# Layer-norm statistics of the mix in a hybrid encoder layer: from bn_stats and a ScalarE normalisation to an accumulator, ScalarE squares and two scalar_tensor_tensor ops

## Chip, cores and metric

The kernel runs on one core of one Trainium2 chip, in float32. The metric is the device time of one execution in microseconds (us). Three runs of the kernel before gave 1359.98, 1362.23 and 1364.86 us; the median is 1362.23 us.

## The reference

One encoder layer over 1536 tokens of width 1024: one sequence of 512 and one of 1024, each with its own conditioning rows (shift, scale, gate). Cut to what matters:

```python
h = x * (1 + sc1) + sh1
mix = token_mixer(h, ...)                         # ends in a product with w_out
x = layer_norm(ALPHA * x + g1 * mix, ln1_g, ln1_b)   # the part that is changed
h = x * (1 + sc2) + sh2
y = hierarchical_moe(h, ...)                      # 32 experts, top-1 group, top-2 experts
return layer_norm(ALPHA * x + g2 * y, ln2_g, ln2_b)

def layer_norm(x, g, b):
    mu = mean(x); xc = x - mu; var = mean(xc * xc)
    return xc * rsqrt(var + LN_EPS) * g + b
```

## The kernel before

The tokens are 12 tiles of 128 rows. Five stages follow one another: conditioning and the first product (to about 325 us), the mix stage that is changed here (about 325 to 516 us), routing tables (to about 560 us), the experts (to about 1275 us), and a last stage that adds the two expert outputs and makes the second layer norm. Every product is split into a high and a low part, so that one float32 product is three matmuls (`three`, L1554 to L1556).

In the mix stage each engine has its own program, and all orders are written out by hand. For tile t:

- **TensorE (PE).** `mix(t)` makes 2 halves (b = 0, 1) of 8 x 3 matmuls of 512 columns each into two PSUM banks; it waits for `z2_l_made`. From tile 2 on, `h2_transposes(t-2)` (L1745) stand between the two halves and wait for `h2_ready`. Behind `mix(t)` comes `route(t-2)` (L1767), which waits for `logit_read`, that is, until VectorE has read the logits of tile t-3. Between `mix(1)` and `mix(2)` stands `edge_mm(6)` (L1649), which sets `fb_made` to 2.
- **VectorE (DVE).** `norm_tile(t)` is `second(t)`, then `low_z(t+2)` (L1255, the low part of the input of `mix(t+2)`), then `x1_out(t)`, then `logits_out(t-2)` (L1328). `second(t)` multiplies both halves by the gate (L1304), adds the residual (L1307, waits for the load of `xr`), takes bn_stats of both halves (L1310), joins them (L1312), adds epsilon (L1314), waits for GpSimd's power, and makes -mean * rstd (L1316, `nmr`).
- **ScalarE (ACT).** `high_z(t+2)` (L881), `normalise(t)` (L938), `copy_h2T(t-1)` (L946).
- **GpSimd (POOL).** `second(t)` makes rstd by a power (L682, one element a row), then waits for x1 and makes h2 = x1 * (1 + sc2) + sh2 in two ops of 1024 elements (L690, L692). Before the first power it waits for `fb_made` to be 2, and between tile 0 and tile 1 it has one more op of 1024 elements (L696).
- **SP (DMA queue).** It loads `xr` of tile t (L531) when the residual of tile t-1 has been taken, and stores h2 and x1 (L535, L537) when h2 is ready. For tile 4, with which the second sequence begins, the load stands behind the stores of tile 3.

The semaphores of the changed part run in this order before: `res_ready` (L1307), `var_ready` (L1314), `rstd_ready` (L682), `shift_ready` (L1316), `res_normed` (L938), `x1_ready` (L1323), `h2_ready` (L692).

The last stage already holds the other form of the same layer norm: L1518 adds the residual with an accumulator, L1520 makes the negative mean, ScalarE squares with that bias (L1063), L1524 makes the variance, GpSimd the power (L776), and L1528 and L1533 normalise.

Of the kernel before, what the change touches and what calls it, by code (L numbers as in the profile page):

```python
# [25 lines left out]
ACT = mybir.ActivationFunctionType  # L26
ALU = mybir.AluOpType
AX = mybir.AxisListType

P = 128  # L30
D = 1024
KD = D // P
# [13 lines left out]
EPS = 1e-5  # L46
ALPHA = 2.0 ** 0.25
# [60 lines left out]
def encoder(nc, ins, outs):  # L108
    ctx = ExitStack()
    with ctx:  # L110
        names = []

        def sem(name):
            names.append(name)
            return ctx.enter_context(nc.semaphore(name))
# [23 lines left out]
        r = Region(W0)  # L139
        win_h = r.take("win_h", [P, KD, 3 * AW], F32R)  # L140
        win_l = r.take("win_l", [P, KD, 3 * AW], F32R)
        r = Region(W0)
# [5 lines left out]
        r = Region(W0)  # L148
# [7 lines left out]
        r = Region(Z0)  # L156
# [7 lines left out]
        r = Region(Z0 + 32 * KB)  # L164
        win_raw = [r.take(f"win_raw{s}", [P, 3 * AW]) for s in range(2)]
        r = Region(C0 + 1312 + 4 * KD * PT * 2)
# [3 lines left out]
        r = Region(Z0 + 24 * KB)  # L170
# [4 lines left out]
        r = Region(Z0)  # L175
        z2T = r.take("z2T", [P, NP, KD, PT])
        r = Region(Z0)
        x1 = r.take("x1", [P, NT, D])

        r = Region(C0)  # L180
# [4 lines left out]
        r = Region(TOP0)  # L185
# [10 lines left out]
        r = Region(C1)  # L196
# [32 lines left out]
        v_rstd = r.take("v_rstd", [P, 1])  # L229
        edge_i = r.take("edge_i", [P, EDGE])  # L230
        edge_w = r.take("edge_w", [P, 2, len(WINDOWS), EDGE])
        stat = r.take("stat", [P, 2, 6])
        mv = r.take("mv", [P, 2])
        rstd = r.take("rstd", [P, 1])
        nmr = r.take("nmr", [P, 1])
# [4 lines left out]
        r = Region(C1)  # L240
# [5 lines left out]
        ln_g = r.take("ln_g", [P, D])  # L246
        ln_b = r.take("ln_b", [P, D])
        w_mid = Region(W0).take("w_mid", [P, KD, 3, AW])
        g1b, sc2b, sh2b = [[b[:].rearrange("p (a n) -> p a n", a=2), w_mid[:, 2 * j:2 * j + 2, 1, :]] for j, b in enumerate((g1b, sc2b, sh2b))]
        xr = Region(XS0).take("xr", [P, D])  # L250
        res = Region(V0).take("res", [P, D])
# [3 lines left out]
        r = Region(C1)  # L255
# [38 lines left out]
        r = Region(C0)  # L294
# [14 lines left out]
        r = Region(W0)  # L309
# [30 lines left out]
        def bcast(row, n):  # L340
# [10 lines left out]
        S = {n: sem(n) for n in (  # L351

            "c_loaded rows_loaded small_loaded sp_rows_loaded wsp_loaded ident_made c_silu cT_made c_ready c_low mod_init"
            " colsT_made cols_ready wspT_made wspT_ready rowsum_made rowsum_ready off_made off_ready"
            " edge_iota spl_ones"

            " x_loaded xT_made x0_ready ada_h_made ada_l_made ada_made mod_hl_made mod_cols mod_made"
            " k_mod k_high k_low win_h_made win_l_made h_ready hT_h_made hT_l_made"
            " late_h_made late_l_made late_made late_row added_h added_l g2_loaded g2_made g2_row g2_added"
# [419 lines left out]
        def _(act):  # L779
# [155 lines left out]

            def normalise(t):
                act.wait_ge(S["shift_ready"], t + 1)
                nc.scalar.activation(res[:], res[:], ACT.Identity, scale=rstd[:, 0:1], bias=nmr[:, 0:1]).then_inc(S["res_normed"], 1)  # L938

            def copy_h2T(t):  # L940

# [6 lines left out]

            high_z(2, 0, 1)
            normalise(0)  # L950
            high_z(3, 1, 1)
            normalise(1)
            copy_h2T(0)
            with act.Fori(1, NT // 2 - 2) as i:
                for s in range(2):
                    high_z(2 * i + s + 2, s, i + 1)
                    normalise(2 * i + s)
                    copy_h2T(2 * i + s - 1)
# [117 lines left out]
        def _(dve):  # L1076
            st = Steps(dve, S["dve_steps"], S["dve_carrier"])
            nv = nc.vector
# [218 lines left out]
            def second(t, s, q):  # L1297

                dve.wait_ge(S["mix_made"], t + 1)
                if not (isinstance(t, int) and t == 0):  # L1300
                    dve.wait_ge(S["x1_ready"], t)
                for b in range(2):
                    c = slice(512 * b, 512 * (b + 1))
                    st.done(nv.tensor_tensor(res[:, c], ps[2 * s + b][:], g1b[q][:, b, :], ALU.mult))  # L1304
                st.sync()
                dve.wait_ge(S["xr_loaded"], 16 * (t + 1))
                nv.scalar_tensor_tensor(res[:], xr[:], ALPHA, res[:], ALU.mult, ALU.add).then_inc(S["res_ready"], 1)  # L1307
                dve.wait_ge(S["res_ready"], t + 1)
                for b in range(2):
                    st.done(nv.bn_stats(stat[:, b, :], res[:, 512 * b:512 * (b + 1)]))  # L1310
                st.sync_apart()
                st.done(nv.bn_aggr(mv[:], stat[:].rearrange("p a b -> p (a b)")))  # L1312
                st.sync()
                nv.tensor_scalar(mv[:, 1:2], mv[:, 1:2], EPS, None, ALU.add).then_inc(S["var_ready"], 1)  # L1314
                dve.wait_ge(S["rstd_ready"], t + 1)
                nv.scalar_tensor_tensor(nmr[:], mv[:, 0:1], -1.0, rstd[:], ALU.mult, ALU.mult).then_inc(S["shift_ready"], 1)  # L1316

            def x1_out(t):
                dve.wait_ge(S["res_normed"], t + 1)
                st.done(nv.tensor_tensor(res[:], res[:], ln_g[:], ALU.mult))  # L1320
                st.sync()
                dst = x1[:, t, :] if isinstance(t, int) else x1[:, bass.ds(t, 1), :].rearrange("p a n -> p (a n)")
                nv.tensor_tensor(dst, res[:], ln_b[:], ALU.add).then_inc(S["x1_ready"], 1)  # L1323

            def logits_out(t):
                dve.wait_ge(S["logit_made"], t + 1)
# [6 lines left out]
            def norm_tile(t, s, q, pair=None, prev=True):  # L1333
                second(t, s, q)
                if pair is not None:
                    low_z(t + 2, s, pair + 1)
                x1_out(t)
                if prev:
                    logits_out(t - 2)
# [5 lines left out]
            norm_tile(3, 1, 0, 1)  # L1345
            dve.wait_ge(S["mod2_loaded"], 16 * 8)
            with dve.Fori(2, NT // 2 - 1) as i:
                st.enter(i - 2, 2 * 6)
                for s in range(2):
                    norm_tile(2 * i + s, s, 1, i)  # L1350
            st.leave(NT // 2 - 3)
# [558 lines left out]
```

## Time and profile before

| | us |
|---|---|
| median of 3 runs (lowest, highest) | 1362.23 (1359.98, 1364.86) |
| time of the profiled execution | 1362.33 |
| its span | 1360.4 |
| PE busy in the span | 1235.3 (91%) |
| PEld (weight load) busy | 1017.7 (75%) |
| DVE busy | 918.5 (68%) |
| ACT busy | 643.7 (47%) |
| POOL busy | 252.3 (19%) |

The span is what the hardware profiler recorded of the program; the execution's own time has 1.9 us more around it. Busy time is an average over all stages, so it doesn't say what a change in one stage is worth: the rows of that stage do. PE is TensorE's matmuls, PEld its weight loads, which run beside them. A timeline row gives the start in us, the time from start to end, the engine, the line, the operation, and in square brackets how long the engine had sat idle and what released it.

### The profile page before, as it was taken

To read this page: it belongs to the slowest core of one execution; us is meant where nothing else is said; L and a number is where in the kernel's file an instruction comes from. 1 tells how busy PE (TensorE), PEld (TensorE's weight loads), DVE (VectorE), ACT (ScalarE), POOL (GpSimd) and SP (SyncE) were. 2 spreads that over 40 slices of the span, in tenths; PEclk is the share of its full clock that TensorE was granted. 3 is DMA by queue.
4 is the path that set the end of the run, shared out by engine and by line. 5 is a ranking of instruction groups with operands and counts; after the bars stand their busy time and mean duration, and the time that the engine had idled before them with its cause. 6 is when DMAs were issued, how large, how long until landed. Compare 5 with 4: busy or idle time off the path is not lost.

```text
span 1360.4 us, 23047 instructions
## 1 busy us (share of the span) xinstructions
PE 1235.3 (91%) x6392; PEld 1017.7 (75%) x6393; DVE 918.5 (68%) x1035; ACT 643.7 (47%) x630; POOL 252.3 (19%) x303
## 2 busy tenths in 40 slices
PE   4989989999999976599999999999999999999490
PEld 3878879998778862478888888888888888888240
DVE  4665655556655556875588657654788888886197
ACT  4543222122121112355577646554787777776121
POOL 0011101001434341111112211111122211222022
PEclk8989989999998986799999999999999999999796
DMA  9743221016232626486699769675899999996983
GB/s 312 227 117 109 79 93 63 16 63 200 75 129 104 241 88 246 156 339 246 230 374 403 307 232 342 252 297 180 325 403 407 397 398 386 404 394 230 380 308 123
DMA packets 120838, 328.98 MB, mean 242 GB/s; under 512 B 12008, under 2 KB 43872, under 8 KB 120804
## 3 DMA queue, kind: packets, MB, share of 16 engines
q1 hardware_dynamic: 106612, 288.08, 57.3%
q0 software_dynamic: 12320, 34.15, 6.8%
q10 hardware_dynamic: 1872, 6.29, 1.1%
q8 instruction: 22, 0.36, 0.1%
q14 instruction: 12, 0.10, 0.0%
HBM read 296.97 MB, written 39.41 MB: 247 GB/s over the span
## 4 chain that ended last, share of the span: by engine, by line
PE 80%; DVE 10%; DMA 3%; issue 2%; ACT 2%; POOL 1%; SPq 0%; POOLq 0%; DVEq 0%; ACTq 0%
PE bank L1554 20%; PE bank L1556 20%; PE bank L1555 20%; PE bank L1567 3%; PE bank L1568 3%; PE bank L1569 3%; PE bank L1817 3%; PE bank L1767 1%; PE bank L1839 1%; DMA y_rows<-y_sb,s_idx 1%; DVE fin L1518 1%; DVE fin L1533 1%; DVE gated L1514 1%; DVE ada_l L1110 1%; PE bank L1608 1%
## 5 line engine op out<-in xcount | busy, mean ns | idle before, releaser
L1453 DVE TENSOR_TENSOR gu_l<-gu_raw,gu_h (+1 forms) x128 | 287.2, 2285 | 41.5 <-ACT gu_h L979 40.8
L1554 PE MATMUL bank<-gu_h,xT_h 128*128 (+1 forms) x624 | 247.6, 397 | 4.1 <-DVE xT_l L1472 4.1
L1556 PE MATMUL bank<-gu_h,xT_l 128*128 (+1 forms) x624 | 244.3, 392 | 0.0
L1555 PE MATMUL bank<-gu_l,xT_h 128*128 (+1 forms) x624 | 244.2, 391 | 0.0
L979 ACT ACTIVATE gu_h<-gu_raw (+1 forms) x128 | 238.5, 1924 | 6.0 <-issue 5.9
L1457 DVE TENSOR_TENSOR dn_l<-dn_raw,dn_h (+1 forms) x64 | 143.6, 2284 | 5.9 <-ACT dn_h L983 5.9
L1554 PEld LDWEIGHTS bank<-gu_h,xT_h 128*128 128x128 f32 x624 | 117.9, 189 | 28.1 <-DVE xT_l L1472 2.9
L1556 PEld LDWEIGHTS bank<-gu_h,xT_l 128*128 128x128 f32 x624 | 117.8, 189 | 24.9
L1555 PEld LDWEIGHTS bank<-gu_l,xT_h 128*128 128x128 f32 x624 | 118.0, 189 | 23.5
L1554 PE MATMUL bank<-dn_h,aT_h 128*128 (+1 forms) x312 | 124.8, 400 | 2.5 <-DVE aT_l L1467 2.5
L983 ACT ACTIVATE dn_h<-dn_raw (+1 forms) x64 | 119.0, 1914 | 10.5 <-DVE table_i L1448 10.4
L1556 PE MATMUL bank<-dn_h,aT_l 128*128 (+1 forms) x312 | 121.8, 391 | 0.0
L1555 PE MATMUL bank<-dn_l,aT_h 128*128 (+1 forms) x312 | 121.6, 390 | 0.0
L1567 PE MATMUL bank<-hT_h,win_h 128*128 128x256 f32 x384 | 111.4, 290 | 8.6 <-ACT z2T L865 4.4
L989 ACT ACTIVATE act_s<-bank 128x512 f32<-128x512 f32 x39 | 23.3, 598 | 181.7 <-PE bank L1556 181.7
L1569 PE MATMUL bank<-hT_h,win_l 128*128 128x256 f32 x384 | 109.1, 284 | 0.0
L1568 PE MATMUL bank<-hT_l,win_h 128*128 128x256 f32 x384 | 109.1, 284 | 0.0
L757 POOL DMA_INDIRECT y_rows<-y_sb,s_idx x39 | 66.9, 1714 | 220.8 <-ACT y_sb L1010 220.8
L1463 DVE TENSOR_TENSOR act_a<-bank,act_s 128x512 f32<-128x512 f32 x39 | 27.0, 691 | 84.0 <-ACT act_s L989 84.0
L1567 PEld LDWEIGHTS bank<-hT_h,win_h 128*128 128x128 f32 x384 | 74.3, 193 | 11.4 <-DVE hT_l L1129 5.9
L1554 PE MATMUL bank<-wout_h,z_h 128*128 128x512 f32 x192 | 79.3, 413 | 2.1 <-DVE z_l L1255 2.1
L1555 PE MATMUL bank<-wout_l,z_h 128*128 128x512 f32 x192 | 77.4, 403 | 0.0
(252 smaller groups left out, 2150.5 us busy)
## 6 DMA issues: line engine op xcount, KB each, us to landing
gu_raw<-in_w_gate_up SPq DMA_DIRECT2D x128, 1024.0 KB, 7.9
dn_raw<-in_w_down SPq DMA_DIRECT2D x64, 1024.0 KB, 7.6
y<-y_rows SPq DMA_DIRECT2D x24, 512.0 KB, 5.0
ada_raw<-in_w_ada SPq DMA_DIRECT2D x20, 512.0 KB, 6.0
ada_raw<-in_w_ada SPq DMA_DIRECT2D x10, 1024.0 KB, 5.3
win_raw<-in_w_in SPq DMA_DIRECT2D x8, 768.0 KB, 8.2
h_rows<-h SPq DMA_DIRECT2D x12, 512.0 KB, 2.7
x_rows<-x SPq DMA_DIRECT2D x12, 512.0 KB, 3.6
```

The lines of the kernel that those rows point to most:

```text
L757: nc.gpsimd.indirect_dma_start(out=y_d, out_offset=bass.IndirectOffsetOnAxis(ap=s_idx[:, 0:1], axis=0), in_=y_sb[:], in_offset=None, bound ...
L979: nc.scalar.activation(gu_slot(gu_h, e, c), gu_slot(gu_raw, e, c), ACT.Copy).then_inc(S["gu_split_h"], 1)
L983: nc.scalar.activation(dn_slot(dn_h, e, c), dn_slot(dn_raw, e, c), ACT.Copy).then_inc(S["dn_split_h"], 1)
L1453: nv.tensor_tensor(gu_slot(gu_l, e, c), gu_slot(gu_raw, e, c), gu_slot(gu_h, e, c).bitcast(F32), ALU.subtract).then_inc(S["gu_split_l"], 1)
L1457: nv.tensor_tensor(dn_slot(dn_l, e, c), dn_slot(dn_raw, e, c), dn_slot(dn_h, e, c).bitcast(F32), ALU.subtract).then_inc(S["dn_split_l"], 1)
L1554: mm(out, lh, rh, start=start, stop=False)
L1555: mm(out, lh, rl, start=False, stop=False)
L1556: return mm(out, ll, rh, start=False, stop=stop)
L1567: mm(out, win_h[:, k, c], hT_h[s][:, k, :], start=start, stop=False)
L1568: mm(out, win_h[:, k, c], hT_l[s][:, k, :], start=False, stop=False)
L1569: return mm(out, win_l[:, k, c], hT_h[s][:, k, :], start=False, stop=stop)
L1817: last = nc.tensor.transpose(ps[2 + k // 4][:, (k % 4) * P:(k % 4 + 1) * P], xg[:, k * P:(k + 1) * P], ident[:])
```

## The change

The residual op L1307 also gives the sum of each row. VectorE makes the negative mean from it; ScalarE no longer normalises but squares the centred rows and gives their sum (its elementwise output goes to an unused part of `w_mid`); `x1_out` makes the variance, normalises in two `scalar_tensor_tensor` ops, (res - mean) * ln_g and then res * rstd + ln_b, and waits for the power between the two. The order of `second`, `low_z`, `x1_out` and `logits_out` stays, and so do the programs of PE, POOL and SP.

```diff
-        stat = r.take("stat", [P, 2, 6])
+        stat = r.take("stat", [P, 2])
...
             def normalise(t):
                 act.wait_ge(S["shift_ready"], t + 1)
-                nc.scalar.activation(res[:], res[:], ACT.Identity, scale=rstd[:, 0:1], bias=nmr[:, 0:1]).then_inc(S["res_normed"], 1)
+                nc.scalar.activation(w_mid[:, KD - 2:KD, 1, :], res[:].rearrange("p (a n) -> p a n", a=2), ACT.Square, bias=mv[:, 0:1], accum_out=stat[:, 1:2]).then_inc(S["res_normed"], 1)
...
-                nv.scalar_tensor_tensor(res[:], xr[:], ALPHA, res[:], ALU.mult, ALU.add).then_inc(S["res_ready"], 1)
+                nv.scalar_tensor_tensor(res[:], xr[:], ALPHA, res[:], ALU.mult, ALU.add, accum_out=stat[:, 0:1]).then_inc(S["res_ready"], 1)
                 dve.wait_ge(S["res_ready"], t + 1)
-                for b in range(2):
-                    st.done(nv.bn_stats(stat[:, b, :], res[:, 512 * b:512 * (b + 1)]))
-                st.sync_apart()
-                st.done(nv.bn_aggr(mv[:], stat[:].rearrange("p a b -> p (a b)")))
-                st.sync()
-                nv.tensor_scalar(mv[:, 1:2], mv[:, 1:2], EPS, None, ALU.add).then_inc(S["var_ready"], 1)
-                dve.wait_ge(S["rstd_ready"], t + 1)
-                nv.scalar_tensor_tensor(nmr[:], mv[:, 0:1], -1.0, rstd[:], ALU.mult, ALU.mult).then_inc(S["shift_ready"], 1)
+                nv.tensor_scalar(mv[:, 0:1], stat[:, 0:1], -1.0 / D, None, ALU.mult).then_inc(S["shift_ready"], 1)
 
             def x1_out(t):
                 dve.wait_ge(S["res_normed"], t + 1)
-                st.done(nv.tensor_tensor(res[:], res[:], ln_g[:], ALU.mult))
+                nv.tensor_scalar(mv[:, 1:2], stat[:, 1:2], 1.0 / D, EPS, ALU.mult, ALU.add).then_inc(S["var_ready"], 1)
+                dve.wait_ge(S["shift_ready"], t + 1)
+                st.done(nv.scalar_tensor_tensor(res[:], res[:], mv[:, 0:1], ln_g[:], ALU.add, ALU.mult))
+                dve.wait_ge(S["rstd_ready"], t + 1)
                 st.sync()
...
-                nv.tensor_tensor(dst, res[:], ln_b[:], ALU.add).then_inc(S["x1_ready"], 1)
+                nv.scalar_tensor_tensor(dst, res[:], rstd[:, 0:1], ln_b[:], ALU.mult, ALU.add).then_inc(S["x1_ready"], 1)
...
-                st.enter(i - 2, 2 * 6)
+                st.enter(i - 2, 2 * 3)
```

## Rows read from the trace of the kernel before

**Rows 1.** Busy time of each engine in two stretches of the mix stage.

```profile
330.00:400.00 70.00, 66.87 (x331) 55.56 (x330) 40.63 (x58) 13.19 (x15) 28.57 (x14) 0.98 0.37 129
...
410.00:470.00 60.00, 60.00 (x300) 50.43 (x301) 33.19 (x48) 13.57 (x16) 25.45 (x14) 0.95 0.44 162
```

**Rows 2.** Timeline of PE, 350 to 417 us.

```profile
350.23 0.50 PE L1554 MATMUL bank<-wout_h,z_h 128*128 128x512 f32 x1 [2.10 <-DVE z_l L1255]
...
358.67 1.09 PE L1745 MATMUL bank<-ident,h 128*128 128x128 f32 x8 [1.03 <-POOL h L692]
...
408.50 2.96 PE L1767 MATMUL bank<-router_w,h2T 128*128 128x36 f32 x16 [1.60 <-DVE logits L1328]
...
411.84 0.63 PE L1555 MATMUL bank<-wout_l,z_h 128*128 128x512 f32 x1
412.27 0.63 PE L1556 MATMUL bank<-wout_h,z_l 128*128 128x512 f32 x1
...
416.08 0.39 PE L1556 MATMUL bank<-wout_h,z_l 128*128 128x512 f32 x1
416.31 0.39 PE L1554 MATMUL bank<-wout_h,z_h 128*128 128x512 f32 x1
```

**Rows 3.** Stretches of 3 us; the granted clock is third from the end.

```profile
351.00:354.00 3.00, 3.00 (x9) 2.30 (x8) 2.96 (x5) 0.27 (x1) 1.08 (x1) 0.53 0.00 0
...
409.00:412.00 3.00, 3.00 (x15) 2.90 (x15) 2.87 (x3) 0.00 (x0) 2.92 (x2) 0.53 0.00 0
```

**Rows 4.** The chain that ended last: start, us, what.

```profile
395.57 4.82 DMA xr<-in_x_sample
...
425.73 1.71 PE bank L1767 x16
```

**Rows 5.** Timeline of DVE in the last tile.

```profile
495.06 1.29 DVE L1304 TENSOR_TENSOR res<-bank,w_mid 128x512 f32<-128x512 f32 x2 [3.74 <-PE bank L1556]
496.38 1.23 DVE L1307 SCALAR_TENSOR_TENSOR res<-xr,res 128x1024 f32<-128x1024 f32 x1
497.64 1.29 DVE L1310 BATCH_NORM_STATS2 stat<-res 128x6 f32<-128x512 f32 x2
...
500.14 0.16 DVE L1316 SCALAR_TENSOR_TENSOR nmr<-mv,rstd 128x1 f32<-128x1 f32 x1 [0.66 <-POOL rstd L682]
...
502.87 1.22 DVE L1323 TENSOR_TENSOR x<-res,ln_b 128x1024 f32<-128x1024 f32 x1
```

**Rows 6.** Timeline of DVE in the last stage, first two tiles.

```profile
1292.76 1.23 DVE L1518 SCALAR_TENSOR_TENSOR fin<-fin,gated 128x1024 f32<-128x1024 f32 x1
1293.91 0.08 DVE L1518 DVE_READ_ACCUMULATOR fin<-fin,gated 128x1 f32 x1
...
1297.52 1.27 DVE L1528 SCALAR_TENSOR_TENSOR fin<-fin,f_mean,ln_gb 128x1024 f32<-128x1024 f32 x1
```

**Rows 7.** Timeline of ACT in the last stage, first tile.

```profile
1294.22 1.15 ACT L1063 ACTIVATE squares<-fin,f_mean 128x1024 f32<-128x1024 f32 x1 [21.89 <-DVE f_mean L1520]
1295.27 0.19 ACT L1063 ACTIVATION_READ_ACCUMULATOR squares<-fin,f_mean 128x1 f32 x1
```

**Rows 8.** Timeline of POOL in tile 0.

```profile
348.28 0.57 POOL L682 TENSOR_TENSOR rstd<-mv,half_neg 128x1 f32<-128x1 f32 x1 [12.27 <-PE bank L1649]
352.92 2.39 POOL L690 TENSOR_TENSOR h<-x,sc2b 128x1024 f32<-128x1024 f32 x1 [4.07 <-DVE x L1323]
355.38 3.23 POOL L692 TENSOR_TENSOR h<-h,sh2b 128x1024 f32<-128x1024 f32 x1
```

**Rows 9.** Timeline of POOL in the last stage, first tile.

```profile
1297.69 1.55 POOL L776 TENSOR_TENSOR f_rstd<-f_varr,half_neg 128x1 f32<-128x1 f32 x1 [23.49 <-DVE f_varr L1524]
```

**Rows 10.** Timeline of DVE in tiles 0 and 1.

```profile
340.01 1.23 DVE L1307 SCALAR_TENSOR_TENSOR res<-xr,res 128x1024 f32<-128x1024 f32 x1
...
348.88 0.16 DVE L1316 SCALAR_TENSOR_TENSOR nmr<-mv,rstd 128x1 f32<-128x1 f32 x1 [5.78 <-POOL rstd L682]
...
354.26 2.13 DVE L1307 SCALAR_TENSOR_TENSOR res<-xr,res 128x1024 f32<-128x1024 f32 x1
```

## Prediction

> **What bounds the kernel now.** I read the busy time by stretches first, because the page's 91% for PE is a mean over stages. In the middle of the mix stage PE is busy for all of 60.00 us; from 330 to 400 us it is idle for 70.00 - 66.87 = 3.13 us [rows 1]. A shorter VectorE chain is worth nothing where PE is full, so the question is where PE waits for that chain. PE's own timeline has three such places before the steady part: 2.10 us for z_l of tile 2, 1.03 us for h2 of tile 0, and 1.60 us for the read logits ahead of route(3) [rows 2]. A fourth place is the tail: behind mix(11) nothing is left for PE but the transposes and the routing of the last tiles, and these wait for x1(11) and h2(11). From there everything hangs on one chain: routing tables, first gather, first expert. In the expert stage PE is the bound again, so whatever the mix stage gains is carried to the end as a shift.
>
> The idle time is not the whole price. After the first and the third wait the granted clock is 0.53 in the next stretch of 3 us, close to the lower of TensorE's two levels, 1.2 GHz [rows 3]. At that level the matmuls of 512 columns start 0.43 us apart, otherwise 0.23 us [rows 2]. After the third wait route(3) takes 2.96 us; a later route takes 1.71 us [rows 4], and about 11 matmuls run 0.20 us late, together some 3.4 us. After the first wait 8 matmuls of that kind stand in the timeline, 1.6 us. After the wait of 1.03 us there is none.
>
> **The tail, term by term.** The last tile shows the chain free of other work. Before, x1(11) is ready at 502.87 + 1.22 = 504.09 us, and the residual op starts at 496.38 us: 7.71 us [rows 5]. The new chain is the one that the last stage already runs on the same shapes. From the start of the residual op to the end of ScalarE's accumulator read it is 1295.27 + 0.19 - 1292.76 = 2.70 us [rows 6, 7]; in it the accumulator's own read costs 0.08 us. Then come the variance, 0.03 us to wake VectorE and about 0.06 us until the gain op may start, and the gain op, 1.27 us [rows 6]. The rsqrt power starts beside the gain op and is not free: it takes 1.55 us there against 0.57 us in the mix stage [rows 8, 9], and ends at 1299.24 us, 0.45 us after the gain op's end at 1298.79 us. So GpSimd got on only when the gain op let it. With 0.03 us to wake up and 1.28 us for the last op (same form as the gain op), the sum is 2.70 + 0.09 + 1.27 + 0.45 + 0.03 + 1.28 = 5.82 us. **The tail gains 7.71 - 5.82 = 1.9 us.** Bounds: a power that isn't held ends before the gain op, and the gain is 2.3 us; one that needs its whole 0.57 us after the gain op leaves 1.8 us.
>
> **What is removed and costs nothing elsewhere.** The two bn_stats, bn_aggr, the epsilon op, the wait for the power and nmr fill 497.64 to 500.30 us, 2.7 us per tile [rows 5]. In tiles 5 to 10 PE covers them; only the tail and the head below pay. ScalarE's op gets 0.1 us longer with its accumulator read (1.15 + 0.19 with an overlap, against 1.25 us), in the same place of its queue; copy_h2T(t-1) behind it waits for transposes that come later anyway. If PE's cover were gone, each tile would still be shorter than before.
>
> **The head: what moves.** The wait for rstd stood ahead of low_z(t+2); now it stands behind it. In tile 0 VectorE sat for 5.78 us in that wait [rows 10], because GpSimd's first power is released by edge_mm(6) only at 348.28 us [rows 8]. Now low_z(2) follows the mean, at about 340.01 + 1.5 = 341.5 us, and mix(2) starts at 350.23 - 2.10 = 348.13 us. Its first half is 24 x 0.233 = 5.6 us, to 353.7 us. Then it needs h2(0). The power of tile 0 stays where it was: rstd at 348.85 us. The gain op is done by then, so the last op ends at 348.88 + 1.28 = 350.2 us, where L690 started at 352.92 us before. GpSimd now runs L690 from 350.3 to 352.7 us. VectorE's residual op of tile 1 comes into it and is held: before, the same op took 2.13 us and ended at 356.39 us, 1.08 us behind the end of L690, and L692, which came next, took 3.23 instead of 2.39 us [rows 8, 10]. The same pattern 2.65 us earlier gives h2(0) at 355.95 us and the transposes at 356.0 us instead of 358.67 us: 2.7 us gained. PE's wait there becomes 356.0 - 353.7 = 2.3 us, longer than the 2.10 us that was followed by the lower clock. I take it that it is followed again, with the 1.6 us of the nearest row. Bounds: nothing, as after 1.03 us, and 3.4 us, as after route(3).
>
> **Where the next stall goes.** Tiles 1 to 3 lose the wait for the power and 1.9 us of chain each. By the same working x1(3) comes some 4 to 5 us earlier than before; with it come h2(3), its stores, and the load of xr(4) that is queued on SP behind them. That load took 4.82 us and ended at 400.39 us [rows 4]; it is what made the logits late for route(3). Now it lands at about 396 us, and 5.8 + 0.2 us later, at about 402 us, the logits are read. PE comes to route(3) 2.7 - 1.6 = 1.1 us earlier than before, at 408.50 - 1.60 - 1.1 = 405.8 us. The logits are 3.5 us ahead of it; the 1.60 us wait and the 3.4 us of low clock behind it go. **The head gains 2.7 - 1.6 + 1.6 + 3.4 = 6.1 us.** Late next is nothing in the steady part: PE is full there, and each tile's chain is shorter than before; the load of xr(9) behind the two large loads of the gate weights also hangs on h2(7), which comes earlier.
>
> **Sum.** 6.1 + 1.9 = 8.0 us. The profiled execution took 1362.33 us (span 1360.4), 0.1 us from the median: 1362.3 - 8.0 = **1354.3 us**.
>
> **A rule against the change.** The rows give the residual op 1.23 us both without an accumulator in the mix stage and with one in the last stage, two float32 sources in SBUF each time [rows 5, 6]. The Trainium skill, in "Vector Engine (DVE) Microarchitecture Reference", section 7, "Points that are easy to get wrong", says that an op of this shape with two SBUF sources that are not bf16 has half the throughput, since no read port is left for the accumulator. The rows do not bear that out; what it would make of the time here is rival E's result instead of A's.
>
> **Rivals.** A, the forecast, with one short drop of the clock: 1354.3 us, chance 0.52.
>
> B, no drop of the clock at the longer wait for h2(0): PE comes to route(3) 1.6 us earlier still, 1352.7 us, chance 0.2. For it speaks that a wait of 1.03 us left the clock alone, against it that waits of 2.10 and 1.60 us didn't.
>
> C, more of the low clock than A has: the drop behind h2(0) costs 3.4 instead of 1.6 us (1356.1 us), or a drop stays at route(3) though its stall has gone (1354.3 + 3.4 = 1357.7 us). For it speaks that the small matmuls of route(3) ran in the slow stretch [rows 3], against it that a later route without a stall took 1.71 us [rows 4]; chance 0.13.
>
> D, the head gives nothing net: xr(4) or the routing still sets route(3), for a reason that I don't see in the rows, and only the tail is left: 1362.3 - 1.9 = 1360.4 us, chance 0.1. Against it stand 3.5 us of slack.
>
> E, on the other side: the three scalar_tensor_tensor ops run at half rate, each 1.23 - 0.16 = 1.07 us longer, with the 0.16 us of the one-element op [rows 10] as the part that doesn't stretch (for the rule, see above; against it 1.23 and 1.27 us [rows 6]). The chain of a tile is then 3.2 - 1.9 = 1.3 us longer than before. In the head h2(0) comes 0.5 us earlier but after a wait of 4.5 us; tile 3 ends 1.2 us later, xr(4) with it, and route(3) starts 2.3 us later; with the tail 3.6 us: 1366 us. It decides from 0.65 us more per op on. Chance 0.05.
>
> **Range and chances.** A has its own range of 1352.5 to 1356 us (the bounds of the clock and of the power). A, B and C hold 0.85; from 1350.5 us, which is B with 2 us for the spread of the runs shown, to 1359.5 us. What a measurement here tells from no change is 0.3%, 4.1 us, so the border is 1358.2 us. A and B and most of C lie below it: faster 0.81; D and the rest of C: same 0.14; E: slower 0.05.
>
> **What the profile after would show.** The three wide VectorE ops at 1.23, 1.27 and 1.28 us (E falls). No wait for z_l at mix(2); a wait of about 2.3 us for h2(0) ahead of the first transposes at about 356.0 us, and the clock behind it (A against B and C). No idle time ahead of route(3), which takes 1.7 us instead of 2.96 us. The power at about 1.5 us instead of 0.57 us, and VectorE waiting 0.5 us for it. The last x1 5.8 us behind the start of its residual op. In the expert stage the same lengths as before, shifted. The prediction is wrong if PE waits at a new place of the mix stage, if ScalarE reloads its function table in the loop for the squares, or if the expert stage doesn't take over the shift.

## The result and the profile after

The changed kernel takes 1349.98 us, the median of 5 runs (1349.51 to 1352.51), against 1362.23 us of the kernel before in the same measurement (5 runs, 1359.26 to 1364.86). The ratio is 0.9917, with a 95% interval of 0.9897 to 0.9936: it is faster, by 11.3 us as the ratio has it. A second measurement of the same kernel (below) gave 0.9929, 9.7 us. The forecast was 1354.3 us, range 1350.5 to 1359.5 us: the direction is right, the median lies half a microsecond below the range (1350.9 us, the ratio times 1362.23 us, lies inside), and the gain was forecast too small.

The page's first part for the changed kernel; columns as before (busy us, share, instructions):

```profile
span 1347.9 us, 23017 instructions
...
PE 1226.7 (91%) x6392; PEld 1012.1 (75%) x6393; DVE 903.4 (67%) x1011; ACT 644.1 (48%) x642; POOL 261.0 (19%) x303
```

VectorE has 15.1 us less work (918.5 to 903.4) and the span is 12.5 us shorter. That the two numbers are near each other means nothing, as the experiments show: in the steady part VectorE's saving isn't what counts.

The same stretches of the mix stage after the change [rows 1]:

```profile
330.00:400.00 70.00, 67.83 (x347) 56.58 (x345) 42.47 (x58) 15.86 (x23) 33.13 (x16) 1.00 0.36 124
...
410.00:470.00 60.00, 60.00 (x310) 50.25 (x309) 27.06 (x42) 14.64 (x22) 27.05 (x13) 1.00 0.48 175
```

The idle time of PE in the first stretch is 70.00 - 67.83 = 2.17 us, all of it one wait, and the granted clock is 1.00 in both. PE's timeline after the change, from edge_mm(6) to the transposes of tile 0, and at route(3) and route(4):

```profile
344.75 0.95 PE L1645 MATMUL bank<-abuf,w_pool 128*128 128x8 f32 x8
345.56 0.47 PE L1550 MATMUL bank<-wout_h,z_h 128*128 128x512 f32 x1
...
353.56 1.09 PE L1741 MATMUL bank<-ident,h 128*128 128x128 f32 x8 [2.17 <-POOL h L692]
...
401.63 1.87 PE L1763 MATMUL bank<-router_w,h2T 128*128 128x36 f32 x16
...
415.48 1.87 PE L1763 MATMUL bank<-router_w,h2T 128*128 128x36 f32 x16
```

The last line is route(4). Before the change it stood here:

```profile
425.56 1.87 PE L1767 MATMUL bank<-router_w,h2T 128*128 128x36 f32 x16
```

Compare with [rows 2]. There is no wait for z_l any more (345.56 follows edge_mm at once), the wait for h2(0) has grown from 1.03 to 2.17 us, and route(3) starts without a wait and takes 1.87 us instead of 2.96 us. The clock ahead of, at and behind the one wait that is left, by stretches of 3 us:

```profile
351.00:354.00 3.00, 0.83 (x6) 0.44 (x5) 2.96 (x4) 1.24 (x2) 3.00 (x2) 1.00 0.00 0
354.00:357.00 3.00, 3.00 (x17) 2.55 (x16) 2.56 (x3) 1.09 (x2) 3.00 (x1) 1.00 0.83 326
357.00:360.00 3.00, 3.00 (x14) 2.41 (x14) 1.29 (x1) 0.00 (x0) 1.09 (x3) 1.00 0.57 198
```

Around this wait it stays at 1.00, the higher of the two levels, 2.4 GHz; before, it was 0.53 after two of the three waits [rows 3].

VectorE in the last tile:

```profile
486.24 1.22 DVE L1307 SCALAR_TENSOR_TENSOR res<-xr,res 128x1024 f32<-128x1024 f32 x1
487.39 0.08 DVE L1307 DVE_READ_ACCUMULATOR res<-xr,res 128x1 f32 x1
487.50 0.15 DVE L1309 TENSOR_SCALAR mv<-stat 128x1 f32<-128x1 f32 x1
488.96 0.15 DVE L1313 TENSOR_SCALAR mv<-stat 128x1 f32<-128x1 f32 x1 [1.31 <-ACT w_mid L938]
489.03 1.28 DVE L1315 SCALAR_TENSOR_TENSOR res<-res,mv,ln_g 128x1024 f32<-128x1024 f32 x1
490.75 1.28 DVE L1319 SCALAR_TENSOR_TENSOR x<-res,rstd,ln_b 128x1024 f32<-128x1024 f32 x1 [0.44 <-POOL rstd L682]
```

From the residual op to x1(11) it is 490.75 + 1.28 - 486.24 = 5.79 us, against 7.71 us before [rows 5]. GpSimd's power of tile 0, which stands alone, and that of tile 11, which runs beside the gain op (L1315):

```profile
345.85 0.57 POOL L682 TENSOR_TENSOR rstd<-mv,half_neg 128x1 f32<-128x1 f32 x1 [12.36 <-PE bank L1645]
...
489.19 1.52 POOL L682 TENSOR_TENSOR rstd<-mv,half_neg 128x1 f32<-128x1 f32 x1 [4.79 <-DVE mv L1313]
```

**Where the time came from.** I cut each trace at the same events: the start of edge_mm(6), the start of the residual op of tile 11, the end of x1(11), the start of the last logits op, the first expert matmul, the first matmul of the last stage, the end. All numbers are differences of timeline entries, in us.

| profiled execution | start of edge_mm(6) | stage: to residual op of tile 11 | to x1(11) | to the last logits | to the first expert matmul | experts | rest |
|---|---|---|---|---|---|---|---|
| before | 347.18 | 149.20 | 7.71 | 11.96 | 54.44 | 714.99 | 74.92 |
| after | 344.75 | 141.49 | 5.79 | 11.95 | 54.61 | 714.70 | 74.61 |
| difference | -2.43 | -7.71 | -1.92 | 0 | +0.2 | -0.3 | -0.3 |

The stage and the tail (from the residual op of tile 11 to x1(11)) give 9.63 us. The stage's 7.71 us can be read off the lines above, from start to start: up to the transposes of tile 0 11.49 - 8.81 = 2.68 us, from there to route(3) 49.83 - 48.07 = 1.76 us (the wait of 1.60 us), and from route(3) to route(4) 17.06 - 13.85 = 3.21 us (the low clock); 0.06 us are left over. The 2.43 us ahead of the stage aren't the change's: there the two kernels run the same work. In the fourteen traces of this case this start lies between 344.75 and 347.18 us.

### The profile page after: what moved, and what is told of

It reads as the page before. It is cut to its first block, busy times and chain, and to the rows that moved or that the text cites. A ratio compares the mean times of both kernels' runs of the same rounds, so it can differ in the third digit from the quotient of the medians.

```text
span 1347.9 us, 23017 instructions
## 1 busy us (share of the span) xinstructions
PE 1226.7 (91%) x6392; PEld 1012.1 (75%) x6393; DVE 903.4 (67%) x1011; ACT 644.1 (48%) x642; POOL 261.0 (19%) x303
## 4 chain that ended last, share of the span: by engine, by line
PE 83%; DVE 8%; DMA 3%; issue 2%; ACT 2%; POOL 1%; SPq 0%; POOLq 0%; DVEq 0%; ACTq 0%
PE bank L1550 21%; PE bank L1552 20%; PE bank L1551 20%; PE bank L1563 3%; PE bank L1564 3%; PE bank L1565 3%; PE bank L1813 3%; PE bank L1763 1%; PE bank L1835 1%; DMA y_rows<-y_sb,s_idx 1%; DVE fin L1514 1%; DVE fin L1529 1%; DVE gated L1510 1%; PE bank L1741 1%; PE bank L1613 1%
## 5 line engine op out<-in xcount | busy, mean ns | idle before, releaser
L1552 PE MATMUL bank<-wout_h,z_l 128*128 128x512 f32 x192 | 75.9, 395 | 0.0
```

The costliest lines, as they stand in the source:

```text
L1552: return mm(out, ll, rh, start=False, stop=stop)
```

## The experiments

My theory: the gain is the head (no wait at mix(2), no stall at route(3)) and the tail, and each needs both parts of the change. The rivals: the gain is spread over all tiles with VectorE's work; the order alone gives it; the statistics alone give it. Of the kernels with one form in some tiles and the other in the rest, only the form differs.

**The changed kernel again** (no edit).

> The changed kernel once more, for a second trace and more times. Theory (head and tail, the clock left to chance): 1350 to 1352 us; the mix stage from the first mix(2) matmul to the last logits as long as in the first trace to within 0.3 us if the clock doesn't drop behind the wait for h2(0), 1.6 us longer if it does; the start of the stage may lie up to 2.5 us elsewhere, since the stage ahead of it is untouched. Rival (the 2.4 us that the first trace had gained ahead of the stage belong to the change): the stage starts at 344.7 us again, within 0.3 us.

1351.68 us, ratio 0.9929 (0.9916 to 0.9942). Start of edge_mm(6) 346.80 us, 2.05 us later than in the first trace of the very same kernel, so that part was chance. Stage 141.48 us, tail 5.80 us, wait for h2(0) 2.16 us with no drop of the clock behind it. Stage and tail repeat to 0.01 us; what differs between runs lies ahead of them and behind them.

**The order alone** (`shift(t)` holds the two lines that are taken out above it).

```diff
                 nv.tensor_scalar(mv[:, 1:2], ..., EPS, None, ALU.add).then_inc(S["var_ready"], 1)
-                dve.wait_ge(S["rstd_ready"], t + 1)
-                nv.scalar_tensor_tensor(nmr[:], ...).then_inc(S["shift_ready"], 1)
...
                     low_z(t + 2, s, pair + 1)
+                shift(t)
                 x1_out(t)
```

> The kernel before with low_z(t+2) ahead of the wait for the power, and nothing else. Theory: the wait of 2.10 us for z_l goes, but h2(0) comes no earlier, so PE waits some 4.9 us for it instead of 2.1 and 1.0; the ScalarE normalisation no longer runs beside low_z, 1.2 us more in each chain, twice on the way to route(3): about 2.4 us slower than before, 1364.6 us. Rival (the moved wait is the gain): about 1358 us, no wait ahead of mix(2) and route(3) some 4 us earlier.

1372.01 us, ratio 1.0078 (1.0065 to 1.0091): 10.6 us slower, not 2.4. The direction was right and the mechanism too, but not its reach. PE's timeline:

```profile
358.57 1.97 PE L1748 MATMUL bank<-ident,h 128*128 128x128 f32 x8 [4.79 <-POOL h L692]
...
412.48 3.51 PE L1770 MATMUL bank<-router_w,h2T 128*128 128x36 f32 x16 [4.39 <-DVE logits L1330]
...
487.07 3.06 PE L1770 MATMUL bank<-router_w,h2T 128*128 128x36 f32 x16 [1.94 <-DVE logits L1330]
```

The 2.10 us wait at mix(2) is gone, and 4.79 us for h2(0) stand in its place. The normalisation now starts behind low_z, so VectorE comes later to the logits of tile 2, which it reads in tile 4, and route(3) waits 4.39 instead of 1.60 us. And there is a wait that I hadn't counted, 1.94 us at 487.07 us. Route(8) stands there; it hangs on xr(9), whose load is queued behind the two large weight loads:

```profile
477.93 1.23 DVE L1307 SCALAR_TENSOR_TENSOR res<-xr,res 128x1024 f32<-128x1024 f32 x1 [5.32 <-DMA xr<-in_x_sample]
```

Each of the three waits is followed by a low clock (0.66, 0.60 and 0.61 in the stretch of 3 us that holds its end); the routes take 3.51 and 3.06 us instead of 1.87. The stage is 158.52 us, 9.3 us longer.

**The statistics alone**, with both waits ahead of low_z.

```diff
                 nv.tensor_scalar(mv[:, 0:1], stat[:, 0:1], -1.0 / D, ...).then_inc(S["shift_ready"], 1)
+                dve.wait_ge(S["res_normed"], t + 1)
+                nv.tensor_scalar(mv[:, 1:2], stat[:, 1:2], 1.0 / D, EPS, ...).then_inc(S["var_ready"], 1)
+                dve.wait_ge(S["rstd_ready"], t + 1)
 
             def x1_out(t):
-                dve.wait_ge(S["res_normed"], t + 1)
...
```

> The new statistics and the two new normalising ops, but with the waits for the squares and for the power kept ahead of low_z(t+2), where the power's wait stood before. Theory (the two parts need each other): tile 0 gains nothing, the waits of 2.1 us for z_l and of 1.0 us for h2(0) come back; the wait ahead of route(3) shrinks but may stay, and the tail gains 1.7 us (the power isn't held): 1357 to 1359.5 us. Rival (the statistics alone carry the gain): 1351 us, the stage from edge_mm to the last residual op at most 143 us instead of 149.2 us.

1359.55 us (12 runs, 1357.42 to 1361.7), ratio 0.9994 (0.9985 to 1.0002): no difference that can be told, and 0.05 us above the range that I expected. The trace has stage 146.88 and tail 6.21 us, together 3.8 us less than before; the times don't show these 3.8 us, and I can't say why. PE:

```profile
349.61 0.50 PE L1551 MATMUL bank<-wout_h,z_h 128*128 128x512 f32 x1 [2.03 <-DVE z_l L1255]
...
357.96 1.91 PE L1742 MATMUL bank<-ident,h 128*128 128x128 f32 x8 [2.50 <-POOL h L692]
```

The wait for z_l is back. So the two parts don't add: order alone 10.6 us slower, statistics alone 0.8 us faster by the ratio and not told from none, both about 10 us faster. The new statistics are what lets low_z move at no cost: the squares run beside low_z (in tile 0 of the changed kernel they end at 340.27 us, low_z at 340.13 us), and only the power is left behind it. That holds for the head. In the tail there is no low_z, and the statistics alone keep 1.50 of its 1.92 us, so there my theory that each gain needs both parts is wrong.

**The new form in the last two tiles alone.**

```diff
-            norm_tile(NT - 2, 0, 1)
-            norm_tile(NT - 1, 1, 1)
+            norm_tile(NT - 2, 0, 1, new=True)
+            norm_tile(NT - 1, 1, 1, new=True)
```

> The new form in tiles 10 and 11 alone, the old one in tiles 0 to 9. Theory: the tail's 1.9 us and nothing of the head: 1360.3 us, route(3) stalls as before at 408.5 us. Rival (the gain of 11.3 us by the ratio is spread over all tiles): also 1360.4 us, but then the steady part between must be shorter too, and the next two runs must come out in proportion to their tiles.

1359.0 us (12 runs), ratio 0.9985 (0.9975 to 0.9995): 2.0 us faster. Tail 5.79 us, stage 149.54 us, route(3) with a wait of 1.90 us.

**The new form in tiles 0 to 5 alone** (the edit of tile 0, repeated for tiles 1 to 5; tiles 6 to 11 as before).

```diff
-            norm_tile(0, 0, 0, 0, prev=False)
+            norm_tile(0, 0, 0, 0, prev=False, new=True)
...
```

> The new form in tiles 0 to 5 alone, the old one in tiles 6 to 11. Theory: the head's whole gain, route(3) without a stall, and the tail as before, 7.71 us from residual op to x1(11): 1.9 us slower than the changed kernel, 1352 to 1353 us. Rival (spread over the tiles): half of 11.3 us, 1356.6 us.

1354.6 us, ratio 0.9952 (0.9939 to 0.9965): 6.5 us faster; 1356.6 us of the rival would be 0.9966 of 1361.21 us, just outside. With the 9.7 us of the second measurement the rival would want 0.9964, just inside, so the time alone doesn't decide. The trace does: stage 141.47 us, as if all twelve tiles had the new form, and tail 7.71 us, as if none had. Route(3) starts without a wait, at normal length:

```profile
402.73 1.87 PE L1790 MATMUL bank<-router_w,h2T 128*128 128x36 f32 x16
```

Tiles 6 to 10 keep VectorE's whole old chain here, and the stage is no longer for it. By its ratio the kernel is 3.1 us behind the changed one, by the profiled executions 2.2 us, where the tail says 1.9.

**VectorE's work put back in the steady part**, in the changed kernel, tiles 4 to 9.

```diff
+                if not isinstance(t, int):
+                    for b in range(2):
+                        st.done(nv.bn_stats(dead[:, b, :], res[:, 512 * b:512 * (b + 1)]))
+                    st.sync()
                 nv.tensor_scalar(mv[:, 0:1], stat[:, 0:1], ...)
```

> The changed kernel with two bn_stats and their wait put back, as unused work, between the residual op and the mean in the six loop tiles 4 to 9 (about 1.5 us per tile on the chain to x1). Theory (PE covers the steady part): no change, 1350 to 1351 us; route(3), which hangs on tile 4, has 2.0 us of slack in the first trace and keeps 0.5 us of it. Rival (VectorE's busy time counts): 6 x 1.5 = 9 us slower, 1359 us.

1350.5 us, ratio 0.9924 (0.991 to 0.9937), stage 141.55 us: the unused work (in tile 4 1.32 us from the first bn_stats to the mean, and so in six tiles) costs nothing, where the rival wanted 9 us. With the runs before, the spread-out gain is refuted. It was close: the logits of tile 2 are read until 402.42 us here, and route(3) starts at about 402.6 us.

**The power ahead of the gain op**, in the changed kernel.

```diff
+                dve.wait_ge(S["rstd_ready"], t + 1)
                 dve.wait_ge(S["shift_ready"], t + 1)
                 st.done(nv.scalar_tensor_tensor(res[:], res[:], mv[:, 0:1], ln_g[:], ALU.add, ALU.mult))
-                dve.wait_ge(S["rstd_ready"], t + 1)
```

> The changed kernel with the wait for the power ahead of the gain op instead of behind it. Theory (the gain op holds the port that the power needs): the power takes 0.55 us instead of 1.52 us; VectorE waits 0.65 us for it, and the tail's chain from the residual op to x1(11) gets 0.1 to 0.2 us longer than 5.8 us; time unchanged within 0.3 us. Rival (the power is slow for another reason, such as cold code): it takes 1.5 us still, the chain is 1.1 us longer, and so is the kernel.

The power takes 0.55 us in all twelve tiles, so the gain op was what held it. The tail is 6.14 us, 0.34 us longer. But the kernel takes 1354.14 us, ratio 0.9946 (0.9932 to 0.9959), some 3 us more than the changed kernel; I had expected no change. The miss is the head: in tile 0 the gain op was hidden in the wait for the power, and now stands behind it.

```profile
347.15 1.28 DVE L1316 SCALAR_TENSOR_TENSOR res<-res,mv,ln_g 128x1024 f32<-128x1024 f32 x1 [5.99 <-POOL rstd L682]
```

PE's wait for h2(0) grows from 2.16 to 3.47 us, and then the clock does fall: 0.58 in the next stretch of 3 us. The stage is 144.34 us, 2.9 us longer: 1.3 us of wait and about 1.55 us of low clock, nearly the 1.6 us that the prediction took for a drop at this place.

**The first power not behind edge_mm(6)**, in the changed kernel; and, in a second kernel, xr(4) also loaded ahead of the stores of tile 3.

```diff
             def second(t, q):
                 pool.wait_ge(S["var_ready"], t + 1)
                 nc.gpsimd.tensor_tensor(rstd[:], ..., ALU.pow).then_inc(S["rstd_ready"], 1)
                 pool.wait_ge(S["x1_ready"], t + 1)
+                if isinstance(t, int) and t == 0:
+                    pool.wait_ge(S["fb_made"], 2)
...
-            pool.wait_ge(S["fb_made"], 2)
             second(0, 0)
```

```diff
-            store_h2(3)
             second(4, 1)
+            store_h2(3)
```

> The changed kernel with GpSimd's wait for edge_mm(6) behind the first power instead of ahead of it, so that only the ops that write h2 wait for it. Theory (the wait for h2(0) hangs on the power at edge_mm): the power runs some 5 us earlier, x1(0) with it, L690 starts when edge_mm is done, and the 2.2 us wait of PE for h2(0) shrinks to 0 or 0.5 us: 2 us faster than the changed kernel, 1348 to 1349 us. Rival (h2(0) is limited by GpSimd's own two ops and the port): less than 1 us.

> The kernel of the run before, and the load of xr(4) queued on SP ahead of the stores of tile 3. Theory: the wait of about 4 us of the residual op of tile 4 for its load goes, but route(3) already has slack in the changed kernel, so nothing on PE moves: same time as the run before within 0.3 us. Rival (the late xr(4) still costs): up to 2 us faster.

1350.21 us, ratio 0.9921 (0.9907 to 0.9934), and 1351.09 us, ratio 0.9925 (0.9912 to 0.9939). In the trace the edit does what it should: the wait for h2(0) is 0.24 us, and the stage 139.56 us, 1.9 us shorter. The load changes nothing on PE, 139.55 us, as expected, though the residual op of tile 4 now waits 0.15 us instead of 4.25 us. Yet the time barely moved: beside the kernel with the dead work, 1350.5 us in the same measurement, the first is 0.3 us faster and the second 0.6 us slower. The expert stage took 715.34 and 715.60 us against 714.24 us in the run with the dead work, which ran on the same chip. In the second 10 us of it, the granted clock was 0.87 instead of 1.00:

```profile
567.70:577.70 10.00, 7.90 (x35) 0.87 0.89 358
```

Here I formed the theory that the lower clock comes with this kernel, and ran it once more.

> The kernel with the early first power once more. Theory (the 1.9 us that the stage gained were taken back by a lower clock at the start of the expert stage, which is the same in each execution of this kernel): stage 139.55 us, the granted clock in the second 10 us of the expert stage below 0.9, time 1350 to 1351 us. Rival (that clock is chance): clock 1.00 there and 1348.5 us.

That theory fell: stage 139.55 us again, but the clock was 1.00 there and the experts took 713.43 us; 1349.22 us (6 runs), ratio 0.9918 (0.9905 to 0.9931). So the lower clock doesn't come with every execution of this kernel. It isn't this kernel's alone either: with each trace cut in the same way, seven of the fourteen have 0.83 to 0.87 in these 10 us, four of them of kernels without the early power (the order alone, the statistics alone, the last two tiles, tiles 0 to 5). Their expert stages take 715.22 to 716.86 us, those of the other seven 713.43 to 716.20 us. Whether the early power makes the lower clock more likely (three of its four traces have it) isn't shown. Nor do the 1.9 us of the stage show in the time: the three ratios, 0.9918 to 0.9925, lie among those of the three measurements with the same tail and without this edit, 0.9917, 0.9924 and 0.9929.

**h2 of the last tile on VectorE**, in the changed kernel, and with the early power as well. `x1_halves` stands for the view of x1(11) in two halves. What is left out of the diff are the waits for x1(11) and for the users of h2(10), and GpSimd's own two ops for tile 11, which are taken out.

```diff
-            norm_tile(NT - 1, 1, 1)
+            second(NT - 1, 1, 1)
+            logits_out(NT - 3)
+            x1_out(NT - 1)
...
+            st.done(nv.tensor_tensor(h2_halves, x1_halves, sc2b[1], ALU.mult))
+            st.sync()
+            nv.tensor_tensor(h2_halves, h2_halves, sh2b[1], ALU.add).then_inc(S["h2_ready"], 1)
```

> The changed kernel with h2 of the last tile made on VectorE (two ops of 1.23 us) instead of GpSimd (2.35 + 2.34 us), and the logits of tile 9 read ahead of x1_out(11), so that route(10) is out of PE's way. Theory (behind mix(11) everything is one chain): the time from x1(11) to the last logits falls from 11.95 us to about 9.4 us and the kernel's with it, 2.5 us faster than the changed kernel. Rival (PE's routing of tile 10 sets the tail): 11.95 us or little less, no change.

> Both found edits together: the first power not behind edge_mm(6), and h2 of the last tile on VectorE. Theory: the stage 1.9 us shorter and the tail 2.5 us shorter than in the changed kernel; how much of it reaches the end depends on the granted clock at the start of the expert stage, 1346 to 1348.5 us. Rival: the expert stage takes back all that the stage gains, 1350 us.

1347.38 us, ratio 0.9906 (0.9891 to 0.9921), and 1346.18 us, ratio 0.9892 (0.9877 to 0.9908). From x1(11) to the last logits it is 9.38 us in both, as expected, instead of 11.95. Two things are moved at once, the two ops and the logits of tile 9, and no run tells their shares. The last is the fastest kernel of this case: 14.7 us less than the kernel before by its ratio (the interval overlaps with that of the kernel without the early power), and its runs (1346.01 to 1348.44) lie below all ten of the changed kernel.

## Why the prediction came out as it did

**The bound and the place of the gain: right.** PE is full from 410 to 470 us before and after, and the dead work put back there costs nothing. Head and tail alone carry the gain, shown by the kernels with the new form in some tiles. None of ScalarE's table loads falls into the stage: the only one between 330 and 520 us stands at 500.29 us (before at 512.35 us), in the routing.

**The tail: right.** Forecast 5.82 us of chain and 1.9 us of gain; measured 5.79 and 1.92. The held power is shown: 1.52 us beside the gain op, 0.55 us when it runs ahead of it. The rule of the Trainium skill in "Vector Engine (DVE) Microarchitecture Reference", section 7, that such an op with two SBUF sources that aren't bf16 has half the throughput for the accumulator's sake, is not borne out: 1.22 us with the accumulator's read of 0.08 us behind it, against 1.23 us without [rows 5]. Rival E fell with it.

**The head's first step: right.** No wait at mix(2), transposes of tile 0 2.7 us earlier (353.56 - 344.75 = 8.81 us after edge_mm(6), before 11.49 us), a wait of 2.3 us forecast and 2.17 us measured. GpSimd's and VectorE's ops held each other in the pattern that I had read from tile 1 (2.14 and 3.21 us against 2.13 and 3.23). Held as well, which I hadn't written, was low_z(3), 3.17 us, but PE doesn't wait for it.

**The step that failed: "I take it that it is followed again, with the 1.6 us of the nearest row."** It isn't: the granted clock stays at 1.00 behind the wait, in all five traces that have it at this length (2.16 or 2.17 us). I had argued from the wait's length (2.3 us, longer than one of 2.10 us that was followed by a drop), and that comparison was with a wait at another place, mix(2); at the transposes of tile 0 the clock fell only behind 2.50 us and more. The size was not what failed: where the clock did fall at this place, behind a wait of 3.47 us, it cost about 1.55 us. So rival B, with a chance of 0.2, is what happened: it gave 1352.7 us, 9.6 us of gain, and stage and tail give 9.63 us. That B's sum agrees so closely is partly luck: two small errors in the price of route(3)'s stall, below, offset each other.

**Where the next stall went: right.** Route(3) starts without a wait, 56.88 us after edge_mm(6) instead of 61.32 us, and the low clock behind it is gone. The logits are read until 399.67 us, 2.0 us ahead of it, where I had 3.5 us. My own figures, 405.8 and about 402 us, give 3.8 us, and PE is there 1.7 us earlier than in forecast A, 1.6 us of it from the clock. The price of the old stall was a little off in both terms: the low clock cost 3.21 us, not 3.4, because I compared route(3) with a length of 1.71 us from a row of the chain, which shows only a part of it, while the timeline has 1.87 us; and the wait put route(3) off by 1.76 us, not 1.60. The sum, 5.0 us, was right.

**The rest of the measured gain.** The first measurement gave 11.3 us, the second 9.7 us, with intervals of about 2.7 and 1.8 us on either side; the 9.63 us lie in both. Differences of about 2 us between runs come from outside the stage in the traces: its start varied by 2.4 us between traces, and the experts took from 713.43 to 716.86 us. My range's lower end took 2 us for that spread below rival B, and the median came out 0.5 us below it.

**What stays open.** What decides if the clock falls behind a wait of 2 us. Why the early power's 1.9 us, and the 3.8 us of the statistics alone, stand in the traces and not in the times: the intervals reach 1.2 to 1.9 us to either side, which may cover the first but not the second.

## What to carry to other kernels

Look for the places where the bounding engine really waits, and cost an edit there and nowhere else: VectorE's old statistics, 2.7 us per tile, cost nothing in tiles 6 to 10. Moving a wait out of the way of one consumer only pays if the next consumer in line comes earlier too: the order alone cost 10.6 us, since it took ScalarE's work out of its cover, and a slack of 0.2 us elsewhere (route(8), behind a large load) turned into a stall. When the bounding engine's clock can fall, a stall has two prices: that of 1.60 us cost 1.76 + 3.21 = 5.0 us, that of 2.17 us only itself. Both belong into the sum as cases, instead of the one that the nearest row shows.

## What the runs showed of the hardware that I had not expected

The length of a wait of PE alone does not tell whether the granted clock falls behind it, and neither does its place alone. At mix(2) it fell behind 2.10 us in both traces that have this wait (0.53 and 0.61 in a stretch of 3 us behind it) and stayed at 1.00 behind 2.03 us in the kernel with the statistics alone. At the transposes of tile 0 it stayed at 1.00 behind 1.03 us in two traces and behind 2.16 to 2.17 us in five, and fell behind 2.50, 3.47 and 4.79 us. At route(3) it fell behind 1.60, 1.90 and 4.39 us and stayed at 1.00 behind 1.04 us; at route(8) it fell behind 1.94 us. So in this stage every wait of 2.50 us or more was followed by a drop, none of 1.04 us or less was, and between 1.60 and 2.17 us it went both ways. Length and place together do sort them: at each place, the waits with a drop behind them are longer than those without, at mix(2) by 0.07 us. These are few waits, and no run varied this alone.

Behind the mix stage the clock is low in both kernels: it is 0.50 from 504 us on before and from 489 us on after, and the last route takes 3.62 to 3.63 us instead of 1.87 us in all fourteen traces. So the 11.95 us from x1(11) to the last logits are spent at the lower of the two levels, 1.2 GHz.

The stage is far more repeatable than the run: 141.47 to 141.55 us in five traces of kernels with the same head, while the time of one kernel spreads over 2 to 3 us.
